# Sparse and forgetting attention: the value products of a half dealt out by key block over the next half's first three tiles

## What is computed

```python
# sparse: the keys that an indexer selects, causal
logits = jnp.einsum('bqhd,bqkd->bqhk', qb, k_sel).astype(jnp.float32) * (HEAD_DIM ** -0.5)
logits = jnp.where(valid[:, :, None, :], logits, -jnp.inf)
p = jax.nn.softmax(logits, axis=-1).astype(v.dtype)
return jnp.einsum('bqhk,bqkd->bqhd', p, v_sel)
...
# forgetting ("fox"): a decay term is added to every logit, causal
s = jnp.einsum('bhqd,bhkd->bhqk', qb, k).astype(jnp.float32)
s = s + fq[..., None] - cum_log_f[:, :, None, :]
s = jnp.where(mask[None, None], s, -jnp.inf)
p = jax.nn.softmax(s, axis=-1)
return jnp.einsum('bhqk,bhkd->bhqd', p.astype(v.dtype), v)
```

## Time and profile before

| | us |
|---|---|
| median of 3 runs | 2185.75 (2183.95 to 2187.93) |
| the profiled execution, time | 2187.79 |
| its span | 2186.0 |
| TensorE matmul busy | 2030.5 (93%) |
| VectorE busy | 1120.3 (51%) |
| GpSimd busy | 1074.1 (49%) |
| ScalarE busy | 728.7 (33%) |
| mean granted clock of TensorE | 0.969 |

### The profile page before, as it was taken

One profiled execution on the slowest core, in us unless ns is written; L12 is line 12 of the kernel. 1 busy time (PEld: TensorE's weight loads), 2 busy tenths in 40 slices (PEclk: granted clock), 3 DMA queues, 4 the chain that ended last, 5 costly groups with the idle time before them and its releaser, 6 DMA issues.

```text
span 2186.0 us, 30713 instructions
## 1 busy us (share of the span) xinstructions
PE 2030.5 (93%) x10091; PEld 1634.9 (75%) x10091; DVE 1120.3 (51%) x1820; ACT 728.7 (33%) x1219; POOL 1074.1 (49%) x615
## 2 busy tenths in 40 slices
PE   8888988979999999766999999999999999999997
PEld 6677766758887888544778888888877778888886
DVE  6788863754777696598333213232227743132232
ACT  4323234344222223444432222233224543222223
POOL 5466325525756644670554444455365435444442
PEclk9999989999999999879999999999989999999999
DMA  4233002222333332100333333333220013333332
GB/s 141 70 96 92 1 1 73 87 49 87 96 98 95 96 93 81 48 1 0 87 96 97 92 100 96 91 96 102 81 77 1 0 39 106 97 97 94 98 95 87
DMA packets 330961, 165.80 MB, mean 76 GB/s; under 512 B 22030, under 2 KB 329606, under 8 KB 330886
## 3 DMA queue, kind: packets, MB, share of 16 engines
q1 hardware_dynamic: 330144, 164.17, 26.2%
q10 hardware_dynamic: 742, 0.68, 0.1%
HBM read 162.48 MB, written 2.10 MB: 75 GB/s over the span
## 4 chain that ended last, share of the span: by engine, by line
PE 59%; issue 12%; POOL 8%; DVE 8%; POOLq 5%; DVEq 4%; ACT 3%; DMA 1%; ACTq 0%; SPq 0%
PE ACC L1339 16%; PE ACC L1345 16%; PE ACC L1340 16%; POOL WL L1004 7%; POOLq L1014 2%; PE ACC L1495 1%; PE O L1461 1%; POOLq L1186 1%; PE FOUR L1461 1%; POOLq L1174 1%; PE O L1462 1%; PE O L1463 1%; ACT WH L492 1%; DMA RAW<-in_w_v_cross_dram 1%; DVEq L2085 1%
## 5 line engine op out<-in xcount | busy, mean ns | idle before, releaser
L1004 POOL TENSOR_TENSOR WL<-RAW,WH 128x1024 fp32r<-128x1024 f32 (+1 forms) x308 | 731.3, 2377 | 790.5 <-ACT WH L492 715.5
L1339 PE MATMUL ACC<-PH,WH 128*128 128x512 f32 x1248 | 494.9, 397 | 8.2 <-DVE PL L1825 2.5
L1340 PE MATMUL ACC<-PL,WH 128*128 128x512 f32 x1248 | 489.3, 392 | 0.0
L492 ACT ACTIVATE WH<-RAW 128x1024 fp32r<-128x1024 f32 (+1 forms) x308 | 317.7, 1033 | 483.7 <-PE ACC L1345 420.4
L1339 PE MATMUL ACC<-QH,WH 128*128 128x512 f32 (+1 forms) x1136 | 431.5, 384 | 20.8 <-ACT WH L492 14.2
L1340 PE MATMUL ACC<-QL,WH 128*128 128x512 f32 (+1 forms) x1136 | 427.1, 380 | 0.0
L1345 PE MATMUL ACC<-PH,WL 128*128 128x512 f32 x1248 | 312.5, 393 | 0.0
L1339 PEld LDWEIGHTS ACC<-PH,WH 128*128 128x128 f32 x1248 | 236.3, 189 | 66.6 <-issue 4.3
L1345 PE MATMUL ACC<-QH,WL 128*128 128x512 f32 (+1 forms) x1136 | 272.0, 380 | 9.6 <-POOL WL L1004 9.4
L1345 PEld LDWEIGHTS ACC<-PH,WL 128*128 128x128 f32 x1248 | 235.3, 189 | 52.8 <-issue 3.3
L1340 PEld LDWEIGHTS ACC<-PL,WH 128*128 128x128 f32 x1248 | 236.3, 189 | 48.9 <-issue 1.0
(11 more groups left out here) (415 smaller groups left out, 2518.9 us busy)
## 6 DMA issues: line engine op xcount, KB each, us to landing
RAW<-in_mlp_w_dram SPq DMA_DIRECT2D x128, 512.0 KB, 4.0
RAW<-in_w_gate_dram SPq DMA_DIRECT2D x22, 512.0 KB, 3.7
RAW<-in_w_up_dram SPq DMA_DIRECT2D x22, 512.0 KB, 3.7
RAW<-in_w_in_dram SPq DMA_DIRECT2D x16, 512.0 KB, 3.8
RAW<-in_w_down_dram SPq DMA_DIRECT2D x16, 512.0 KB, 3.9
RAW<-in_ssm_w_glu_dram SPq DMA_DIRECT2D x16, 512.0 KB, 3.9
RAW<-in_w_kvf_dram SPq DMA_DIRECT2D x16, 512.0 KB, 3.9
RAW<-in_w_k_cross_dram SPq DMA_DIRECT2D x8, 512.0 KB, 4.0
```

The source lines that it names most:

```text
L492: act.activation(WH[:, s, 0:kc], RAW[:, s, 0:kc], ACT.Copy).then_inc(w_hi, 1)
L1004: pool.tensor_tensor(WL[:, s, 0:kc], RAW[:, s, 0:kc], WH[:, s, 0:kc], ALU.subtract).then_inc(w_lo, 1)
L1339: pe.matmul(ACC[s][:, 0:n], WH[:, s, k, :], xh[:, k, :], start=(k == 0), stop=False)
L1340: pe.matmul(ACC[s][:, 0:n], WH[:, s, k, :], xl[:, k, :], start=False, stop=False)
```

## The change

The 12 value products of a half are no longer one run. `values` takes a list of key blocks, and the new table `BLOCKS` gives block 0 to the first tile of the next half, block 1 to the second, blocks 2 and 3 to the third and none to the fourth; the call is made at every tile. `pv_done` is now counted for every block (8 to a group, not 2), `turned_high` of query block qb waits for block qb alone, and the readout of `O` moves two tiles back: `out_high` from t = 0 to t = 2, `out_low` from t = 1 to t = 3. The cross attention keeps its order; only its counts shift. The last half of a stage, inside `first_projected`, stays one run of 12.

```diff
+VALUES = {"sparse": 1, "cross": 33, "fox": 41}
+BLOCKS = ((0,), (1,), (2, 3), ())
...
@@ turned_high (ScalarE)
-                if qb == 0:
-                    act.wait_ge(pv_done, HALVES[kind] + 2 * c + t // TB)
+                if kind == "cross":
+                    if qb == 0:
+                        act.wait_ge(pv_done, VALUES[kind] + 2 * c)
+                elif not (isinstance(c, int) and c == 0 and t < TB):
+                    act.wait_ge(pv_done, VALUES[kind] + 8 * c + 4 * (t // TB) - 3 + qb)
...
@@ attend (ScalarE)
-                        if t == 0 and not first:
+                        if t == (0 if kind == "cross" else 2) and not first:
                             out_high(kind, c - 1)
...
@@ values (TensorE)
-                for k in range(TB):
-                    mm = three(O[:, k * P:T], vh[:, k, half, :], vl[:, k, half, :], PTH[:, k, k * P:T],
-                               PTL[:, k, k * P:T], half == 0 and k == 0, half == 1 and k == TB - 1)
-                mm.then_inc(pv_done, 1)
+                for k in blocks:
+                    three(O[:, k * P:T], vh[:, k, half, :], vl[:, k, half, :], PTH[:, k, k * P:T],
+                          PTL[:, k, k * P:T], half == 0 and k == 0, half == 1 and k == TB - 1).then_inc(pv_done, 1)
...
@@ attend (TensorE; attend_sparse in the same way)
-                        if t == 0 and not first:
-                            values(kind, c - 1, 1 - b, halves - 1)
-                        if t == TB:
-                            values(kind, c, b, 0)
+                        if kind == "cross":
+                            if t == 0 and not first:
+                                values(kind, c - 1, 1 - b, 0)
+                        elif t >= TB:
+                            values(kind, c, b, 0, BLOCKS[t - TB])
+                        elif not first:
+                            values(kind, c - 1, 1 - b, 1, BLOCKS[t])
...
@@ attend (VectorE; attend_sparse in the same way)
-                        if t == 1 and not first:
+                        if t == (1 if kind == "cross" else 3) and not first:
                             out_low(kind, c - 1)
```

More of the change, by code:

```diff
@@ L92 @@
 STAGED = {"sparse": 0, "cross": 4, "fox": 8}
-HALVES = {"sparse": 1, "cross": 9, "fox": 17}
+VALUES = {"sparse": 1, "cross": 33, "fox": 41}
+BLOCKS = ((0,), (1,), (2, 3), ())
 def constants():
@@ L432, in _ @@
                     sp.wait_ge(cvs_in, 4)
-                    sp.wait_ge(pv_done, HALVES["cross"] + 6)
+                    sp.wait_ge(pv_done, VALUES["cross"] + 6)
                     for ri, x in enumerate(("ssm_b_re_2", "ssm_b_im_2")):
@@ L476, in _ @@
             loads("wo", 8, w_o)
-            sp.wait_ge(pv_done, HALVES["fox"] + 16)
+            sp.wait_ge(pv_done, VALUES["fox"] + 64)
             sp.dma_start(YGAIN[:], A["final_norm_2"].rearrange("(o d) -> o d", o=1).to_broadcast([P, D])).then_inc(y_gain, 16)
@@ L642, in out_high @@
                     high_out((O, ST)[m], OUT[kind][0][:, chunk, :],
-                             HALVES[kind] + 2 * c + (m + 1 if kind == "cross" else 2))
+                             VALUES[kind] + (2 * c + m + 1 if kind == "cross" else 8 * c + 8))
             def values_high(kind, c, b):
@@ L717, in attend_sparse @@
                         turned_high("sparse", c, t)
-                        if t == 0 and c:
+                        if t == 2 and c:
                             out_high("sparse", c - 1)
@@ L1496, in turn, with values @@
                 mm.then_inc(t_ready, 1)
-            def values(kind, c, b, half):
+            def values(kind, c, b, half, blocks=range(TB)):
                 pe.wait_ge(pt_lo, TILES[kind] + SIZE[kind] * c + 4 * half + 6)
@@ L1541, in attend @@
                 size, ahead = SIZE[kind], AHEAD[kind]
-                halves = size // TB
                 def group(c, b, first, last):
@@ L1610, in attend_sparse @@
                         turn("sparse", c, t)
[L1611 to L1614, removed]
+                        if t >= TB:
+                            values("sparse", c, b, 0, BLOCKS[t - TB])
+                        elif c:
+                            values("sparse", c - 1, 1 - b, 1, BLOCKS[t])
                         if n == CONV_END[1] + 3:
@@ L2163, in attend_sparse @@
                             low_tile(n - 1)
-                        if t == 1 and c:
+                        if t == 3 and c:
                             out_low("sparse", c - 1)
```

## The result

| | before | after |
|---|---|---|
| median (range), us | 2186.13 (2183.95 to 2187.93) | 2208.87 (2208.15 to 2210.45), 4 runs each |
| profiled execution: time, span | 2187.79, 2186.0 | 2208.15, 2206.3 |
| mean granted clock | 0.969 | 0.956 |
| first scores of fox | 1628.40 | 1624.84 |
| last turn of fox | 1768.45 | 1789.60 |

The changed kernel takes 1.0105 times as long (95% interval 1.0089 to 1.0121): 22.7 us slower. The forecast was 2250 us with a range of 2185 to 2266. So the sign and the range held, and the size did not: 64 us were forecast. It is rival 2, the clock that comes back in the middle of fox.

What follows compares the result with a forecast made beforehand. TensorE, busy 93% of the span, was taken as the bound. 2187.8 + 69 (fox at half clock) - 5 (sparse stage) = 2251.8 us for the profiled execution, 2.0 above the median, so 2250; range 2185 to 2266.

Steps and rivals of the forecast that it cites:

- rival 2: Full clock comes back in the middle of fox, each group earlier giving 10.4 us back: 2188 to 2240 us; chance 0.15.
- The term of 69 us: Fox at half clock from first value product to last turn: 192.4 us against 123.2, costing 69 us (66 to 73).
- Stalls at full clock: Fox: TensorE's waits of 0.45 and 0.21 us a group vanish, plus last-group waits; saves up to 5.6 us.
- Calls and register waits: Added `values` calls in fox's loop cost at most 0.7 to 1.1 us a group, 4 to 7 us in all.
- Readout two tiles later: `out_low` ahead of the `PTL` of t = 3 can bring a stall back: 0 to 0.7 us a group.
- Sparse stage: Less time at half clock and shorter last waits at the stage's end: 5 us saved, bounds 0 and 8.
- Rival 3: Full clock is there; added calls and `out_low` outweigh the saved stalls in fox: 2184 to 2192 us; chance 0.08.
- Rival 1: Clock comes back in fox as before, through the shorter runs: 2176 to 2184 us, middle 2180; chance 0.17.
- The forecast also fails if TensorE no longer stands before fox: Start of fox: without TensorE's pause it would enter the stage at full clock; no size given.

Runs made afterwards that it cites:

- e1: Changed kernel, but the first half of fox's group 0 keeps its 12 value products in one run; 2178.43 us.
- e2: Changed kernel plus nine unread dense matmuls behind key block 0 in fox's first group; 2177.89 us.
- e11: Changed kernel, but fox's first group deals the value products of half 0 as two runs of six; 2177.04 us.
- e12: Changed kernel plus three unread dense matmuls behind key block 0 in fox's first group; 2176.77 us.
- e4: Changed kernel, but the sparse stage has the order of before, so only fox is dealt out; ten runs, 2179.92 to 2215.63 us.
- e9: e1 without the empty fourth call, and with the waits of `values` only in the call that opens a half; 2180.42 us.
- e10: Changed kernel plus 8 unread dense matmuls ahead of the query projection before fox; 2177.44 us.
- e3: Changed kernel, but fox has the order of before, so only the sparse stage is dealt out; 2187.21 us.
- e15: Changed kernel plus 12 unread dense matmuls ahead of the query projection before fox; 2175.23 us.
- e5: Changed kernel plus 20 unread dense matmuls just ahead of fox, 16 before the wait for the gates and 4 before the first scores; 2175.99 us.
- e7: Kernel before, with its order of value products, plus 20 unread dense matmuls just ahead of fox; 2183.21 us.
- e13: The changed kernel itself, nothing altered, timed again; 2206.49 us, one of its five runs at 2195.00.
- e14: Changed kernel plus 4 unread dense matmuls ahead of the query projection before fox; 2177.35, 2179.01, 2180.99, 2210.45 and 2212.00 us.

## Why the prediction was right in sign and wrong in size

- **What raises the clock.** Right in the main: a busy TensorE with scores and turns does not do it, and cutting the unbroken run of 128-row products takes away what did it each time. The 90.00 busy us at 0.50 and e1, e2, e11 and e12 show it. The Trainium skill, "TensorE: Matmul & The Clock Gate", section "What's actually happening", says that activity releases the throttle; for activity as the profile's busy time the trace speaks against it.
- **The step that failed**: "Nothing in the new order is as dense as what raised the clock before. So I expect it to stay at 1.2 GHz from 1628 us to the output projection." The run of block 0 with the transposes behind it can raise the clock, so the clock came back at 1723.9 us and not in the output projection. The term of 69 us was thereby mis-sized. Up to the rise its parts are right, 26.81 us a group where 26.8 was forecast. From the fourth of these runs (1722.16) to the last turn its parts give 13.8 + 3 x 26.8 + 13.0 + 5.0 = 112.2 us, and 67.4 were measured (to 1789.60), 44.8 less; 69.2 - 44.8 = 24.4 is near the +24.7 of fox.
- **The chances.** I read the rows of before as one rule and gave rival 2 only 0.15. They held one case of each kind, and e4's ten runs show that the length of the half clock isn't fixed by the kernel. In the earlier trace rows 249.8 to 253.3 looked like a proof against a short run; it was one draw.
- **Stalls at full clock**: forecast up to 0.66 us in each loop group. Measured are 16.13 to 16.16 us a loop group in e1, e9 and e10, where the kernel before takes 16.40 to 16.44: 0.27. The step to the turn of t = 2 lost 0.30 of its 0.45 us; the wait for `PTL` at t = 0 stayed (0.19 us, 0.21), so that part was wrong. The last group gave what was forecast, some 1 us: its two turns waited 1.08 and 0.59 us before, one of them 0.58 us in e10.
- **Calls and register waits**: 4 to 7 us at the most were booked as possible, the traces of e1 and e9 show none.
- **Readout two tiles later**: booked with 0 to 0.7 us a group for a later `PTL` of t = 3, and this is there, but small: the values of t = 4 start 0.47 to 0.50 us behind their transpose, 0.36 to 0.37 before. `out_low` takes 692 ns in the profile after too.
- **`turned_high`**: its wait was to fall from 28.8 us in 118 us of fox to a few. In e1, at full clock, it is 23.7 us in 112 (1650 to 1762 us), in more and shorter waits (28, the longest 1.1 us, not 4.9): it waits for a block's products at every tile now. It lies on no bound, as said.
- **Sparse stage**: -5 forecast (0 to -8), -4.7 at the last turn and -3.6 at fox's start in the profiles; by itself (e3) 2.2 us, with an interval that reaches zero; in its trace fox, with the order of before, gave the 3 us back.
- **Rival 3** ends here. **Rival 1** is what e10 and e15 show: 2176 to 2184 forecast, 2175 to 2177 measured. The profiled executions of e10 and before differ by 11.1 us. Fox starts 3.7 us earlier (1624.66) and takes 133.60 us, 6.5 less; 0.9 is behind it. Of the 6.5, 2.7 are the second fall of before, which doesn't come (the group with it takes 19.11 us, not 16.42), 1.9 are the six loop groups, 1.5 the last group, and 0.3 group 0.
- "The forecast also fails if TensorE no longer stands before fox" was wrong as a reason: in e5 and e7 it hardly stood (0.57 and 0.58 us), and the clock fell some 3.4 us into the scores.

What stays open is why a run of three raises the clock in one execution and not in another. The traces narrow it. In all seven where a run of three came ahead of the rise (after, e4, e5, e10, e13, e14, e15), it was one of t = 4, with the four transposes of the next values right behind it, and the clock rose 1.6 to 3.3 us after its start. In three of these traces eight such runs passed without a rise, and so did all eight runs of t = 0 at half clock, which have scores behind them. The transposes may thus be part of what raises the clock; no run takes them away or moves them.

## What to carry to other kernels

Before cutting up or moving TensorE's dense runs, look where the granted clock rises and what ran right ahead of it: a stage of scores over 64 rows and transposes may live off one run of 6 to 12 matmuls over all 128 rows, and here one such run, in the stage's first group, gave the dealt-out order both its shorter waits and its clock. Time a change near such a place in several versions, with a few matmuls added ahead: here the same edit measured +22.7 us, or -10.7 us with eight unread matmuls that lay some 67 us ahead of the deciding place. And where one row of the trace speaks against a rival, count how many such rows there are before the chance is given.

## What the runs showed of the hardware

- TensorE can be busy for 90.00 of 90.00 us, as the profile counts it, and be granted 0.50 throughout (after, 1630 to 1720 us).
- The full clock can fall while TensorE works: in e7 at 1630, some 3.3 us into the scores, which stand 0.58 us behind 20 dense matmuls.
- Once up, the clock held through runs of three products: 117 us at 1.00 in e1. No trace with fox in the changed order shows a second fall in the stage (14 traces); each of the three with the order of before does (at 1693.5, e3 at 1690.2, e7 at 1705.3).
- The moment of the rise differs from run to run of one kernel: ten runs of e4 span 2179.92 to 2215.63 us, while the kernel before stayed within 2186.37 to 2194.13 in 20 runs on the same chip. The Trainium skill, "TensorE: Matmul & The Clock Gate", section "What's actually happening", notes that a warm-up varies between runs of one kernel and counts it as a small share of a span; here two runs of one kernel lie 36 us apart, 1.6% of the time.
